# Two heads share two tiles by halves in a float32 encoder kernel

## The chip, the core and the metric

The kernel runs on one core of one Trainium2 chip. TensorE (PE in the profile; PEld is its weight load) multiplies, VectorE (DVE) and ScalarE (ACT) do the elementwise work, SyncE (SP) issues the transfers, GpSimd (POOL) does nothing here. Each engine runs its own list of instructions in order and waits on semaphores. The metric is the time of one execution on the device in microseconds (us), lower is better.

## The reference, cut to what matters

```python
for i in range(DEPTH):                       # DEPTH = 2 layers, 16 + 256 tokens, width 2048
    h = rms_norm(x, norm_w)
    proj = jnp.einsum('bld,dn->bln', h, w_in)            # one projection for all groups
    ya = diff_attention(aq, ak, av, ...)                 # branch A: 4 heads, two maps each
    yb = axial_gqa(bq, bk, bv, ...)                      # branch B: 4 q heads, 2 kv heads
    yc = latent_attention(cq, ckv, ckr, ...)             # branch C: low-rank latents
    yd = multiscale_pool(du, d_w_group, d_scale)         # branch D
    y = concat([ya * silu(ag), yb * silu(bg), yc * silu(cg), yd * silu(dg)])
    x = x + jnp.einsum('bln,nd->bld', y, w_out)

def axial_gqa(...):                          # heads of 128
    q, k = rms_norm(q_raw, q_norm_w), rms_norm(k_raw, k_norm_w)
    # rotary by halves: 0:64 by the grid row, 64:128 by the grid column;
    # apply_rope pairs element d with element d + 32 of its half (the partner)
    q, k = axial(q), axial(k)
    p = softmax32(q @ k, scale);  o = p @ v              # two q heads per kv head

def latent_attention(...):
    c_q, c_kv = rms_norm(cq_raw, q_lat_w), rms_norm(ckv_raw, kv_lat_w)
    q, kv = c_q @ w_uq, c_kv @ w_ukv                     # 4 heads, 128 nope + 64 rope
    q_nope, k_nope = rms_norm(q[..., :128], ...), rms_norm(kv[..., :128], ...)
    s = q_nope @ k_nope + q_rope @ k_rope                # then softmax and v
```

## The kernel before

Everything is kept transposed: features on the 128 partitions, the 272 tokens (`L`; 256 for queries and gates of the last layer) along the row. The big products (input projection, latent up-projections, output projection) are split by hand into a high and a low part of each factor, and `three` (lines 626 to 630) issues three matmuls for each product. Their weights come in chunks; ScalarE makes `w_hi` (`split`, L886), VectorE `w_lo` (`split`, L1162), three chunks ahead of TensorE. One chunk is 24 of these matmuls. A layer has 129 chunk slots: 23 column pairs of the input projection (4 slots each), 5 slots of up-projection behind the fourth pair, 8 output pairs.

A column pair of the projection gives two tiles of 128 features. ScalarE copies each out of PSUM (`lift`, L909), VectorE multiplies it by the inverse root of its token (`rescale`, L1170). Most tiles go to the two-tile buffer `row`. Then, for every tile with a norm of its own (`aq`, `ak`, `bq`, `bk`, and in branch C `qn`, `kn`, `qr`, `kr`):

- `rope_pre` on ScalarE squares the tile (`sq`, L949) and, for those that rotate, copies it with the norm weight (`qw`, L952);
- `rope_stat` on TensorE sums the squares over the partitions by a plain float32 matmul with a matrix of ones (`norm_ps`, L719) and, for those that rotate, fetches each element's partner by a matmul with a permutation (`swap_ps`, L724);
- `rope_fin` on ScalarE forms the inverse root (`rn`, L975 and L976), on VectorE rotates (L1182 to L1184) and multiplies by `rn` (L1191, or L1193 for `qn` and `kn`, which do not rotate).

The two latents are normalised by `lat_pre` (L959), `lat_stat` (L733: 3 matmuls for `cq`, 2 for `ckv`), `lat_fin` (L1206) and then split into `y_hi` (ScalarE, L1004) and `y_lo` (VectorE, L1200). A score step (`score`) makes two maps of 128 queries (or 16) by 272 keys. In branch A each map contracts 64 partitions (L764), m = 0 the lower half of the partitions and m = 1 the upper; in B each contracts 128 (L766); in C 128 (L768) and then 64 for the rotary part (L772). VectorE takes the maximum (L1273), ScalarE the exponential (L1039), VectorE divides (L1289, L1290), TensorE transposes (`p_turn`, L788) and multiplies by the values (`pv`, L807).

The order on each engine is written out by `make_plan`: a stage gets the number of a slot plus a fraction from a table of its engine (`AT_TENSOR`, `AT_SCALAR`, `AT_VECTOR`), and the engine runs its stages sorted by this sum. On TensorE `chunk` stands at 0.5 and `rope_stat` at 0.6, so a statistic of slot s follows the chunk of slot s, and the chunk of slot s + 1 is queued behind it. The latents' statistics stand at slots 12 and 13, those of `qn` 0, `kn` 0, `qr` 0, `qn` 1, `kn` 1, `qn` 2, ... from slot 22 on, one in each slot. Gates (`gate`: L1237, L1238, L1240) stand on VectorE at 0.336.

## Time and profile before

| | us |
|---|---|
| median of 3 runs | 961.72 (960.15 to 962.0) |
| the profiled execution, its time | 962.08 |
| its span in the profile | 960.3 |
| TensorE busy in it | 933.7 |
| VectorE busy in it | 689.0 |
| ScalarE busy in it | 577.9 |

The profiled execution lasted 0.4 us more than the median, and 1.8 us of it lie outside the span. TensorE's busy time has no large gap in any of 40 slices but the first and, a little, the last, and the granted clock is full in nearly all of them. An instruction of TensorE that is recorded as lasting 0.29 us is pipelined with its neighbours: what counts is the distance from one start to the next. A plain float32 matmul is recorded as two instructions.

### The profile page before, as it was taken

What the parts mean: (1) busy time and instruction counts of PE and PEld (TensorE: products, weight loads), DVE (VectorE), ACT (ScalarE), POOL (GpSimd) and SP (SyncE); (2) the same over time, 40 slices, a digit from 0 to 9 for tenths busy, and PEclk for the clock granted to TensorE, in tenths of its full rate; (3) what the DMA queues carried; (4) which work ended last, traced back from release to release, by engine and by line L of the source; (5) the groups of instructions that cost most, each with busy time, mean ns of one, the idle gap of its engine ahead of it and who ended that gap; (6) DMA issues with size and microseconds to landing.
All of it is one profiled execution on the core that took longest, in us unless ns stands there. A gap on an engine that the chain in (4) does not pass through costs nothing.

```text
span 960.3 us, 18378 instructions
## 1 busy us (share of the span) xinstructions
PE 933.7 (97%) x7144; PEld 891.2 (93%) x7144; DVE 689.0 (72%) x1100; ACT 577.9 (60%) x1038; POOL 0.2 (0%) x4
## 2 busy tenths in 40 slices
PE   6999999999999999999999999999999999999998
PEld 6998988999999989899999999999999999999998
DVE  6866986678687688876665568776787868787453
ACT  7577766557576665555554677665586575654331
POOL 0000000000000000000000000000000000000000
PEclk9999999999999999999999999999999999999999
DMA  9535332433333333344555354234434334334552
GB/s 345 218 133 189 119 130 89 136 128 132 132 132 132 132 114 125 114 176 175 177 187 176 132 176 176 92 129 146 148 125 154 132 133 172 126 111 174 200 181 91
DMA packets 22710, 143.84 MB, mean 150 GB/s; under 512 B 2528, under 2 KB 4576, under 8 KB 6240
## 3 DMA queue, kind: packets, MB, share of 16 engines
q1 hardware_dynamic: 22624, 142.67, 41.4%
q8 instruction: 57, 0.93, 0.4%
q14 instruction: 29, 0.24, 0.1%
HBM read 140.56 MB, written 2.10 MB: 149 GB/s over the span
## 4 chain that ended last, share of the span: by engine, by line
PE 83%; DVE 10%; ACT 5%; issue 1%; DMA 1%; SPq 0%; ACTq 0%; DVEq 0%
PE dense L628 23%; PE dense L630 23%; PE dense L629 23%; PE o_ps L807 4%; DVE gate_e L1238 3%; DVE w_lo L1162 3%; PE norm_ps L719 3%; PE swap_ps L724 2%; ACT w_hi L886 1%; PE t_ps L788 1%; PE s_ps L764 1%; PE s_ps L768 1%; ACT h_hi L867 1%; DVE stat L1273 1%; PE s_ps L772 1%
## 5 line engine op out<-in xcount | busy, mean ns | idle before, releaser
L628 PE MATMUL dense<-h_hi,w_hi 128*128 128x272 f32 (+1 forms) x1472 | 441.5, 300 | 11.8 <-DVE h_lo L1142 9.4
L630 PE MATMUL dense<-h_hi,w_lo 128*128 128x272 f32 (+1 forms) x1472 | 424.4, 288 | 0.0
L629 PE MATMUL dense<-h_lo,w_hi 128*128 128x272 f32 (+1 forms) x1472 | 422.4, 287 | 0.0
L1162 DVE TENSOR_TENSOR w_lo<-raw,w_hi 128x1024 fp32r<-128x1024 f32 (+1 forms) x258 | 314.5, 1219 | 73.7 <-ACT w_hi L886 66.8
L886 ACT ACTIVATE w_hi<-raw 128x1024 fp32r<-128x1024 f32 (+1 forms) x258 | 272.4, 1056 | 72.0 <-PE dense L630 62.2
L628 PEld LDWEIGHTS dense<-h_hi,w_hi 128*128 128x128 f32 x1472 | 279.4, 190 | 16.0 <-issue 10.6
L629 PEld LDWEIGHTS dense<-h_lo,w_hi 128*128 128x128 f32 x1472 | 279.8, 190 | 1.8
L630 PEld LDWEIGHTS dense<-h_hi,w_lo 128*128 128x128 f32 x1472 | 278.9, 189 | 0.0
L628 PE MATMUL dense<-y_hi,w_hi 128*128 128x272 f32 (+1 forms) x564 | 163.1, 289 | 3.6 <-DVE y_lo L1200 2.6
L630 PE MATMUL dense<-y_hi,w_lo 128*128 128x272 f32 (+1 forms) x564 | 162.6, 288 | 0.0
L629 PE MATMUL dense<-y_lo,w_hi 128*128 128x272 f32 (+1 forms) x564 | 162.2, 288 | 0.0
L628 PEld LDWEIGHTS dense<-y_hi,w_hi 128*128 128x128 f32 x564 | 108.0, 191 | 4.7 <-DVE y_lo L1200 3.0
L630 PEld LDWEIGHTS dense<-y_hi,w_lo 128*128 128x128 f32 x564 | 108.1, 192 | 0.0
L629 PEld LDWEIGHTS dense<-y_lo,w_hi 128*128 128x128 f32 x564 | 107.9, 191 | 0.0
L909 ACT ACTIVATE row<-dense 128x272 f32<-128x272 f32 (+1 forms) x80 | 31.5, 393 | 47.5 <-PE dense L630 46.2
L1238 DVE RECIPROCAL gate_e<-gate_e 128x272 f32<-128x272 f32 (+1 forms) x32 | 57.7, 1803 | 1.1
L975 ACT ACTIVATE rn<-norm_ps,eps_c 128x272 f32<-128x272 f32 (+1 forms) x64 | 31.0, 484 | 44.2 <-PE swap_ps L724 17.3
L1004 ACT ACTIVATE y_hi<-yt 128x256 fp32r<-128x256 f32 (+2 forms) x36 | 14.4, 400 | 69.5 <-DVE yt L1227 41.2
L1170 DVE TENSOR_TENSOR row<-row,rinv 128x272 f32<-128x272 f32 (+1 forms) x80 | 35.0, 437 | 25.5 <-ACT row L909 23.5
L807 PE MATMUL o_ps<-p_t,v_st 128*128 128x128 f32 (+1 forms) x360 | 47.3, 276 | 4.3 <-ACT p_t L1054 4.3
L807 PEld LDWEIGHTS o_ps<-p_t,v_st 128*128 128x128 f32 x360 | 45.2, 194 | 6.4 <-ACT p_t L1054 5.3
L1273 DVE TENSOR_REDUCE stat<-s_ps 128x1 f32<-128x272 f32 (+1 forms) x80 | 35.1, 439 | 21.8 <-PE s_ps L764 16.6
...
## 6 DMA issues: line engine op xcount, KB each, us to landing
raw<-w_stream_dram SPq DMA_DIRECT2D x128, 1024.0 KB, 4.8
...
con<-consts_dram SPq DMA_DIRECT2D x1, 320.0 KB, 12.7
...
```

Of the source, the lines that this page charges most:

```text
L628: nc.tensor.matmul(ps, whi, xhi, start=first, stop=False)
L629: nc.tensor.matmul(ps, whi, xlo, start=False, stop=False)
L630: return nc.tensor.matmul(ps, wlo, xhi, start=False, stop=last)
L719: sums = nc.tensor.matmul(norm_ps[:, t0:L], halves if width == 64 else ones, sq[:, parity("rope_stat", l, key, i), t0:L], start=True, stop ...
L807: mm = nc.tensor.matmul(o_ps[:, c:c + nq], v_st[:, b, 128 * vh:128 * vh + 128], p_t[:, m, 128 * b:128 * b + nq], start=b == 0, stop=b == 2)
L886: signal(nc.scalar.activation(w_hi[:, g % RING, 0:n], raw[:, e % RAW, CHUNK * half:CHUNK * half + n], ACT.Copy), hi_ready, g + 1)
L909: signal(nc.scalar.activation(tile_place(l, p, j), ps[:, 0:L - tile_from(l, kind)], ACT.Copy), lifted, scaled_no[(l, p, j)])
L975: link(nc.scalar.activation(rn[:, t0:L], norm_ps[:, t0:L], ACT.Ln, scale=1.0 / width, bias=eps_c[:, 0:1]))
L1162: signal(nc.vector.tensor_tensor(w_lo[:, g % RING, 0:n], raw[:, e % RAW, CHUNK * half:CHUNK * half + n], w_hi[:, g % RING, 0:n].bitcast(F3 ...
L1170: signal(nc.vector.tensor_tensor(out_, out_, rinv[:, tile_from(l, PAIRS[p][0]):L], ALU.mult), scaled, scaled_no[(l, p, j)])
L1238: link(nc.vector.reciprocal(e, e))
L1273: link(nc.vector.reduce_max(stat[0:nq, m:m + 1], s_ps[m][0:nq, 0:L], AX.X))
```

## The change

Two heads share two tiles by halves. For branch B and for `qn` and `kn` of branch C, the columns of the weights are reordered so that the first tile of a pair holds the first half of both heads (64 partitions each) and the second tile the second half; in B the halves are chosen so that an element and its rotary partner stand on the same partition of the two tiles. The two query heads that share a pair in B are 0 with 2 and 1 with 3 (`B_HEAD_AT`), one for each kv head. It follows:

- the partner matmul of B goes (`qw` and `swap_ps` too): VectorE rotates out of `row`, both tiles at once (`rope_mid`, three instructions over 2 x 272 columns);
- each pair has one square on ScalarE over both tiles, VectorE adds the two squared tiles (`sq_sum`), and one matmul with `halves` gives the sums of both heads. TensorE waits for the sum (semaphore `summed`) and no longer for the square. The latents' squares are added by VectorE too, two additions for `cq`, one for `ckv`, and one matmul each is left;
- `rope_fin` is one for each pair; in C its product stays two instructions;
- a score of B or C contracts 64 partitions at a time: the map of one head takes the lower half of the partitions of both tiles, the other the upper half. B has four such products in a step where it had two of 128, C six where it had two of 128 and two of 64;
- the list of C's stages is shorter (6 slots where it had 10). `sq_sum` stands at 0.2 of VectorE's table and `rope_mid` at 0.25; all other numbers stay;
- to make room, `gate_e` lies in `c_st[:, 4]` (a gate waits for the split of `ckv`), `acc` in `pooled`, and `sq` has four tiles. The lift behind `bq` and `bk` waits for `rotated`.

```diff
...
-AT_VECTOR = dict(s_max=-0.418, lam_dot=-0.35, sub_fin=-0.345, rope_fin=-0.34, lat_fin=0.055, head_out=0.17,
+AT_VECTOR = dict(sq_sum=0.2, rope_mid=0.25, s_max=-0.418, lam_dot=-0.35, sub_fin=-0.345, rope_fin=-0.34, lat_fin=0.055, head_out=0.17,
...
-                if kind in ("aq", "ak", "bq", "bk"):
+                if kind in ("aq", "ak"):
                     at(s, ("rope_pre", l, kind, i0 + j, j))
                     at(s, ("rope_stat", l, kind, i0 + j))
                     at(s + 1, ("rope_fin", l, kind, i0 + j))
+                elif kind in ("bq", "bk"):
+                    if j == 0:
+                        at(s, ("rope_pre", l, kind, i0 // 2, None))
+                        at(s, ("sq_sum", "rope", l, kind, i0 // 2))
+                        at(s, ("rope_mid", l, kind, i0 // 2))
+                        at(s, ("rope_stat", l, kind, i0 // 2))
+                        at(s + 1, ("rope_fin", l, kind, i0 // 2))
...
             at(s + n, ("lat_pre", l, key))
+            at(s + n, ("sq_sum", "lat", l, key))
             at(s + n, ("lat_stat", l, key))
             at(s + n + 1, ("lat_fin", l, key))
...
-        posts = [("qn", 0), ("kn", 0), ("qr", 0), ("qn", 1), ("kn", 1),
-                 ("qn", 2), ("kn", 2), ("qr", 1), ("qn", 3), ("kn", 3)]
+        posts = [("qn", 0), ("kn", 0), ("qr", 0), ("qn", 1), ("kn", 1), ("qr", 1)]
         for n, (key, i) in enumerate(posts):
             s = g0 + pair_slot(4) + 1 + n
             at(s, ("rope_pre", l, key, i, None))
+            if key in PAIRED:
+                at(s, ("sq_sum", "rope", l, key, i))
             at(s, ("rope_stat", l, key, i))
             at(s + 1, ("rope_fin", l, key, i))
...
-    sq = sb("sq", [128, 3, L])
+    sq = sb("sq", [128, 4, L])
     qw = sb("qw", [128, 2, L])
     rn = sb("rn", [128, L])
-    ta = sb("ta", [128, L + 16])
-    tb = sb("tb", [128, L + 16])
-    gate_e = sb("gate_e", [128, L])
+    tab = sb("tab", [128, 2, L + 16])
+    ta, tb = tab[:, 0, :], tab[:, 1, :]
+    gate_e = c_st[:, 4, :]
     pooled = sb("pooled", [128, L])
     probs = sb("probs", [128, 2, 2, L])
     p_t = sb("p_t", [128, 2, 3 * 128])
-    acc = sb("acc", [128, L])
+    acc = pooled
...
+    def pair_target(key, i):
+        return (q_st if key in ("bq", "qn") else k_st)[:, 2 * i:2 * i + 2, :]
+    def pair_source(key, i):
+        return row[:, :, 8:8 + L] if key in ("bq", "bk") else pair_target(key, i)
+    def twice(a, n):
+        return a.unsqueeze(1).broadcast_to([128, 2, n])
...
         def rope_stat(l, key, i):
-            branch, width = rope[key]
+            branch, _ = rope[key]
             t0 = rope_from(l, key)
-            pe.wait_ge(pre_done, pre_no[("rope_pre", l, key, i)])
+            if key in PAIRED:
+                pe.wait_ge(summed, sum_no[("rope", l, key, i)])
+            else:
+                pe.wait_ge(pre_done, pre_no[("rope_pre", l, key, i)])
             norm_free("rope_stat", l, key, i)
-            sums = nc.tensor.matmul(norm_ps[:, t0:L], halves if width == 64 else ones,
-                                    sq[:, parity("rope_stat", l, key, i), t0:L],
+            sums = nc.tensor.matmul(norm_ps[:, t0:L], halves, sq[:, 2 * parity("rope_stat", l, key, i), t0:L],
                                     start=True, stop=True)
             if branch:
                 swap_free("rope_stat", l, key, i)
             sums.then_inc(stat_done, 1)
         def lat_stat(l, key):
-            pe.wait_ge(pre_done, pre_no[("lat_pre", l, key)])
+            pe.wait_ge(summed, sum_no[("lat", l, key)])
             norm_free("lat_stat", l, key)
-            n = 3 if key == "cq" else 2
-            for k in range(n):
-                mm = nc.tensor.matmul(norm_ps[:, 0:L], ones, sq[:, k, :], start=k == 0, stop=k == n - 1)
-            mm.then_inc(stat_done, 1)
+            nc.tensor.matmul(norm_ps[:, 0:L], ones, sq[:, 0, :], start=True, stop=True).then_inc(stat_done, 1)
...
-            for m in (0, 1):
-                ps = s_ps[m][0:nq, 0:L]
-                if branch == "a":
-                    half = slice(64 * m, 64 * m + 64)
-                    mm = nc.tensor.matmul(ps, q_st[half, h, q:q + nq], k_st[half, h, :], start=True, stop=True)
-                elif branch == "b":
-                    mm = nc.tensor.matmul(ps, q_st[:, h + m, q:q + nq], k_st[:, h // 2, :], start=True, stop=True)
-                else:
-                    nc.tensor.matmul(ps, q_st[:, h + m, q:q + nq], k_st[:, h + m, :], start=True, stop=False)
+            if branch == "a":
+                parts = [(q_st[:, h, :], k_st[:, h, :])]
+            else:
+                k0 = h if branch == "c" else 0
+                parts = [(q_st[:, h, :], k_st[:, k0, :]), (q_st[:, h + 1, :], k_st[:, k0 + 1, :])]
             if branch == "c":
+                parts.append((c_st[:, 6 + h // 2, :], c_st[:, 5, :]))
+            for n_part, (queries, keys) in enumerate(parts):
                 for m in (0, 1):
                     half = slice(64 * m, 64 * m + 64)
-                    mm = nc.tensor.matmul(s_ps[m][0:nq, 0:L], c_st[half, 6 + h // 2, q:q + nq], c_st[half, 5, :],
-                                          start=False, stop=True)
+                    mm = nc.tensor.matmul(s_ps[m][0:nq, 0:L], queries[half, q:q + nq], keys[half, :],
+                                          start=n_part == 0, stop=n_part == len(parts) - 1)
             mm.then_inc(scores_ready, 1)
...
+                    elif pk in ("bq", "bk"):
+                        act.wait_ge(rotated, mid_no[(prev[0], pk, pi // 2)])
...
-            if key in ("qn", "kn", "qr"):
-                pass
-            else:
+            if key in ("bq", "bk"):
+                for t in (0, 1):
+                    act.wait_ge(scaled, scaled_of(l, key, 2 * i + t))
+            elif key not in ("qn", "kn", "qr"):
                 act.wait_ge(scaled, scaled_of(l, key, i))
             buffers_free("rope_stat", l, key, i)
             half = parity("rope_stat", l, key, i)
+            if key in PAIRED:
+                signal(nc.scalar.activation(sq[:, 2 * half:2 * half + 2, t0:L], pair_source(key, i)[:, :, t0:L],
+                                            ACT.Square), pre_done, pre_no[("rope_pre", l, key, i)])
+                return
             src = rope_source(key, i, j)[:, t0:L]
...
+            act.wait_ge(y_ready, y_count[(l, "ckv")])
...
+        def sq_sum(what, l, key, i=None):
+            n = sum_no[(what, l, key) if i is None else (what, l, key, i)]
+            if what == "lat":
+                dve.wait_ge(pre_done, pre_no[("lat_pre", l, key)])
+                if key == "cq":
+                    link(nc.vector.tensor_tensor(sq[:, 1, :], sq[:, 1, :], sq[:, 2, :], ALU.add))
+                signal(nc.vector.tensor_tensor(sq[:, 0, :], sq[:, 0, :], sq[:, 1, :], ALU.add), summed, n)
+                return
+            t0, half = rope_from(l, key), parity("rope_stat", l, key, i)
+            dve.wait_ge(pre_done, pre_no[("rope_pre", l, key, i)])
+            a, b = sq[:, 2 * half, t0:L], sq[:, 2 * half + 1, t0:L]
+            signal(nc.vector.tensor_tensor(a, a, b, ALU.add), summed, n)
+        def rope_mid(l, key, i):
+            t0 = rope_from(l, key)
+            n = L - t0
+            out_, t = pair_target(key, i)[:, :, t0:L], tab[:, :, t0:L]
+            tables = con[:, CC["neg_b"]:CC["neg_b"] + 3 * L].rearrange("p (a t) -> p a t", a=3)
+            x1, x2 = (twice(row[:, j, 8 + t0:8 + L], n) for j in (0, 1))
+            free = max(store_free(l, "b", key[-1], 2 * i + j) for j in (0, 1))
+            if free:
+                dve.wait_ge(scores_ready, free)
+            link(nc.vector.scalar_tensor_tensor(t, x1, pcol(l, key, 0), tables[:, 1:3, t0:L], ALU.mult, ALU.mult))
+            signal(nc.vector.scalar_tensor_tensor(out_, x2, pcol(l, key, 1), tables[:, 0:2, t0:L],
+                                                  ALU.mult, ALU.mult), rotated, mid_no[(l, key, i)])
+            link(nc.vector.tensor_tensor(out_, out_, t, ALU.add))
+        def pair_fin(l, key, i):
+            t0 = rope_from(l, key)
+            out_ = pair_target(key, i)[:, :, t0:L]
+            dve.wait_ge(rn_ready, norm_order[("rope_stat", l, key, i)] + 1)
+            if key in ("bq", "bk"):
+                last = nc.vector.tensor_tensor(out_, out_, twice(rn[:, t0:L], L - t0), ALU.mult)
+            else:
+                for j in (0, 1):
+                    o = out_[:, j, :]
+                    last = nc.vector.scalar_tensor_tensor(o, o, pcol(l, key, j), rn[:, t0:L], ALU.mult, ALU.mult)
+                    if j == 0:
+                        link(last)
+            signal(last, fin_done, fin_no[("rope_fin", l, key, i)])
...
-    put("cos_b", np.concatenate([cr, cc]))
-    put("sin_b", np.concatenate([sr, sc]))
+    put("cos_b", np.concatenate([cr[:32], cc[:32]] * 2))
+    put("sin_b", np.concatenate([sr[32:], sc[32:]] * 2))
+    put("neg_b", np.concatenate([sr[:32], sc[:32]] * 2))
...
+            elif kind in ("bq", "bk", "bg"):
+                heads = [wi[:, :, OFF[kind] + 128 * h:OFF[kind] + 128 * h + 128]
+                         for h in ((0, 1) if kind == "bk" else B_HEAD_AT[i:i + 2])]
+                cols = np.concatenate(heads if kind == "bg" else [h[:, :, d] for d in B_HALVES for h in heads], axis=2)
...
```

What this moves on VectorE is read at three places. In all of them `sq<-sq` (L1213, L1214, L1219) is the sum that TensorE waits for.

First place: VectorE at the two latent norms of layer 0 (slots 12 and 13), before: the latents' rescale, two chunks' `w_lo`, the product of `cq`, its low part, a chunk, the same for `ckv`.

```order
L1170 TENSOR_TENSOR c_st<-c_st,rinv 128x272 x2
L1162 TENSOR_TENSOR w_lo<-raw,w_hi 128x1024 x2
L1206 SCALAR_TENSOR_TENSOR c_st<-c_st,par,rn 128x272 x3
L1200 TENSOR_TENSOR y_lo<-c_st,y_hi 128x816
L1162 TENSOR_TENSOR w_lo<-raw,w_hi 128x768
L1206 SCALAR_TENSOR_TENSOR c_st<-c_st,par,rn 128x272 x2
L1200 TENSOR_TENSOR y_lo<-c_st,y_hi 128x544
```

The same place after:

```order
L1204 TENSOR_TENSOR c_st<-c_st,rinv 128x272 x2
L1196 TENSOR_TENSOR w_lo<-raw,w_hi 128x1024
L1213 TENSOR_TENSOR sq<-sq 128x272
L1214 TENSOR_TENSOR sq<-sq 128x272
L1196 TENSOR_TENSOR w_lo<-raw,w_hi 128x1024
L1283 SCALAR_TENSOR_TENSOR c_st<-c_st,par,rn 128x272 x3
L1277 TENSOR_TENSOR y_lo<-c_st,y_hi 128x816
L1214 TENSOR_TENSOR sq<-sq 128x272
L1196 TENSOR_TENSOR w_lo<-raw,w_hi 128x768
L1283 SCALAR_TENSOR_TENSOR c_st<-c_st,par,rn 128x272 x2
L1277 TENSOR_TENSOR y_lo<-c_st,y_hi 128x544
```

Two additions stand behind the first `w_lo`, the sum for `ckv` behind the low part of `cq`, which itself waits for ScalarE's `y_hi`.

Second place: VectorE at the norms of `qn` 0 and `kn` 0 in layer 0 (slots 21 to 23), before: a gate, a chunk, then products and chunks in turn.

```order
L1237 TENSOR_SCALAR gate_e<-gate_e 128x272
L1238 RECIPROCAL gate_e<-gate_e 128x272
L1240 TENSOR_TENSOR g_st<-row,gate_e 128x272
L1162 TENSOR_TENSOR w_lo<-raw,w_hi 128x1024
L1193 SCALAR_TENSOR_TENSOR q_st<-q_st,par,rn 128x272
L1162 TENSOR_TENSOR w_lo<-raw,w_hi 128x1024
L1193 SCALAR_TENSOR_TENSOR k_st<-k_st,par,rn 128x272
L1162 TENSOR_TENSOR w_lo<-raw,w_hi 128x1024
```

After, with the gate's buffer now in `c_st`:

```order
L1314 TENSOR_SCALAR c_st<-c_st 128x272
L1315 RECIPROCAL c_st<-c_st 128x272
L1317 TENSOR_TENSOR g_st<-row,c_st 128x272
L1196 TENSOR_TENSOR w_lo<-raw,w_hi 128x1024
L1219 TENSOR_TENSOR sq<-sq 128x272
L1246 SCALAR_TENSOR_TENSOR q_st<-q_st,par,rn 128x272 x2
L1196 TENSOR_TENSOR w_lo<-raw,w_hi 128x1024
L1219 TENSOR_TENSOR sq<-sq 128x272
L1246 SCALAR_TENSOR_TENSOR k_st<-k_st,par,rn 128x272 x2
L1196 TENSOR_TENSOR w_lo<-raw,w_hi 128x1024
```

Each sum stands behind a chunk's `w_lo`, and that behind the two products of the pair before.

Third place: VectorE at `bk` in layer 1 (and alike at the first `bq` of layer 1), before: rescale, the end of a head of branch A (L1216, L1218), a chunk, the low part of that head, the rotation.

```order
L1170 TENSOR_TENSOR row<-row,rinv 128x272 x2
L1216 SCALAR_TENSOR_TENSOR ta<-o_ps,sub_w,rn 128x256
L1218 TENSOR_TENSOR yt<-ta,g_st 128x256
L1162 TENSOR_TENSOR w_lo<-raw,w_hi 128x1024
L1200 TENSOR_TENSOR y_lo<-yt,y_hi 128x256
L1182 TENSOR_TENSOR ta<-swap_ps,con 128x272
L1183 TENSOR_TENSOR tb<-qw,con 128x272
L1184 TENSOR_TENSOR tb<-tb,ta 128x272
L1191 TENSOR_TENSOR k_st<-tb,rn 128x272
L1162 TENSOR_TENSOR w_lo<-raw,w_hi 128x1024
```

After:

```order
L1204 TENSOR_TENSOR row<-row,rinv 128x272 x2
L1293 SCALAR_TENSOR_TENSOR tab<-o_ps,sub_w,rn 128x256
L1295 TENSOR_TENSOR yt<-tab,g_st 128x256
L1196 TENSOR_TENSOR w_lo<-raw,w_hi 128x1024
L1277 TENSOR_TENSOR y_lo<-yt,y_hi 128x256
L1219 TENSOR_TENSOR sq<-sq 128x272
L1231 SCALAR_TENSOR_TENSOR tab<-row,par,con 128x2x272
L1232 SCALAR_TENSOR_TENSOR k_st<-row,par,con 128x544
L1234 TENSOR_TENSOR k_st<-k_st,tab 128x544
L1242 TENSOR_TENSOR k_st<-k_st,rn 128x544
```

The sum takes the place of the rotation's first instruction, behind the chunk and the head's low part. For the other four pairs of B the sum stands directly behind a chunk.

## Rows read from the trace of the kernel before

**Rows 1.** The page: span, and busy time of the engines.
```profile
span 960.3 us, 18378 instructions
...
PE 933.7 (97%) x7144; PEld 891.2 (93%) x7144; DVE 689.0 (72%) x1100; ACT 577.9 (60%) x1038; POOL 0.2 (0%) x4
...
```

**Rows 2.** The page, chain that ended last: shares of the span.
```profile
...
PE 83%; DVE 10%; ACT 5%; issue 1%; DMA 1%; SPq 0%; ACTq 0%; DVEq 0%
...
```

**Rows 3.** Chain in order of time: start, us, engine, tile, line, instructions merged.
```profile
...
53.16 1.37 PE norm_ps L733 x6
...
86.58 0.46 PE norm_ps L719 x2
...
107.92 0.92 PE s_ps L768 x4
108.84 0.66 PE s_ps L772 x4
109.50 0.66 PE norm_ps L719 x2
...
```

**Rows 4.** Timeline, latent norms, layer 0: start, us, engine, line [idle before <-releaser].
```profile
...
51.83 1.23 DVE L1162 TENSOR_TENSOR w_lo<-raw,w_hi 128x1024 fp32r<-128x1024 f32 x1 [0.66 <-ACT w_hi L886]
...
53.00 1.54 PE L733 MATMUL norm_ps<-sq,con 128*128 128x272 f32 x6
...
57.36 0.88 ACT L1004 ACTIVATE y_hi<-c_st 128x816 fp32r<-128x816 f32 x1 [1.07 <-DVE c_st L1206]
57.40 1.08 PE L733 MATMUL norm_ps<-sq,con 128*128 128x272 f32 x4
...
58.34 1.01 DVE L1200 TENSOR_TENSOR y_lo<-c_st,y_hi 128x816 fp32r<-128x816 f32 x1 [1.08 <-ACT y_hi L1004]
...
```

**Rows 5.** Timeline, a gate and the norms of qn and kn, layer 0.
```profile
...
84.01 1.85 DVE L1238 RECIPROCAL gate_e<-gate_e 128x272 f32<-128x272 f32 x1
...
86.38 1.23 DVE L1162 TENSOR_TENSOR w_lo<-raw,w_hi 128x1024 fp32r<-128x1024 f32 x1
86.42 0.62 PE L719 MATMUL norm_ps<-sq,con 128*128 128x272 f32 x2
...
88.18 0.50 DVE L1193 SCALAR_TENSOR_TENSOR q_st<-q_st,par,rn 128x272 f32<-128x272 f32 x1 [0.58 <-ACT rn L976]
...
88.72 1.23 DVE L1162 TENSOR_TENSOR w_lo<-raw,w_hi 128x1024 fp32r<-128x1024 f32 x1
...
89.90 0.62 PE L719 MATMUL norm_ps<-sq,con 128*128 128x272 f32 x2
...
```

**Rows 6.** Timeline, first tile of bk, layer 1.
```profile
...
756.02 0.73 PE L719 MATMUL norm_ps<-sq,con 128*128 128x272 f32 x2 [0.15 <-ACT qw L952]
756.03 1.22 DVE L1162 TENSOR_TENSOR w_lo<-raw,w_hi 128x1024 fp32r<-128x1024 f32 x1
...
757.29 0.42 DVE L1200 TENSOR_TENSOR y_lo<-yt,y_hi 128x256 fp32r<-128x256 f32 x1
...
```

**Rows 7.** Stretches: each engine's busy us (instructions), then PEclk, DMA share, GB/s.
```profile
...
374.00:380.00 6.00, 4.66 (x35) 4.11 (x34) 5.69 (x10) 3.33 (x8) 0.00 (x0) 1.00 0.51 178
399.50:401.50 2.00, 0.17 (x2) 0.00 (x0) 1.90 (x4) 1.57 (x6) 0.00 (x0) 1.00 0.01 4
...
404.00:406.00 2.00, 2.00 (x11) 2.00 (x10) 1.24 (x5) 1.31 (x3) 0.00 (x0) 0.50 0.51 213
406.00:408.00 2.00, 2.00 (x14) 2.00 (x13) 1.97 (x2) 0.41 (x1) 0.00 (x0) 0.75 0.00 0
...
```

**Rows 8.** Groups by form: instructions, busy us, mean ns, idle before.
```profile
...
L1184 DVE TENSOR_TENSOR tb<-tb,ta 128x272 f32<-128x272 f32 x24 | 10.6, 442 | 0.8
...
L1193 DVE SCALAR_TENSOR_TENSOR k_st<-k_st,par,rn 128x272 f32<-128x272 f32 x8 | 4.0, 502 | 6.8 <-ACT rn L976 6.8
...
L1105 DVE TENSOR_TENSOR q_st<-q_st 128x544 f32<-128x544 f32 x1 | 0.7, 728 | 0.0
...
```

**Rows 9.** Waits in total, TensorE: us, times, longest.
```profile
...
PE t_ps L788 <- DVE probs L1290: 2.5, 2, 1.3
...
```

76 lines of the change are left out of this document (43 added, 33 removed).

## The prediction, made before the changed kernel was run

> **What bounds the kernel now.** I read the page first: TensorE is busy for 933.7 of 960.3 us, and the chain of work that ended last lies on it for 83% of the span [rows 1, 2]. VectorE has 72%. So a microsecond of TensorE is worth a microsecond of time, nearly everywhere, and so is a microsecond in which TensorE is made to wait. I then read the chain in order of time for the prices of the small matmuls, the timeline for where VectorE stands when TensorE reaches a statistic, and the windows for the places where TensorE has waited before. The reader should see in the timeline rows that ScalarE's squares are ready when TensorE comes: its statistic follows its chunk with no idle time but once, 0.15 us [rows 4 to 6]. VectorE is at that moment in the middle of a `w_lo` of 1.23 us, or about to begin one. That is the place where the new sum comes in.
>
> **Prices on TensorE.** Three float32 matmuls of 128 by 272 take 1.37 us in the chain, a single one 0.46 us [rows 3]. A pair of half-height matmuls, m = 0 and m = 1, costs 0.66 us; the statistic behind it then takes 0.66 us in place of 0.46, so a pass of halves costs 0.66 + 0.20 = 0.86 us, which I split into 0.46 us for the pass (the two halves run beside each other) and 0.40 us for going in and out of that mode [rows 3].
>
> **What goes on TensorE.** Latents: `cq` 3 to 1 matmuls, `ckv` 2 to 1, 3 x 0.46 = 1.4 us a layer. Branch C: 8 statistics become 4, 4 x 0.46 = 1.8 us a layer. Branch B: a pair had 4 matmuls (two statistics, two partners) and has 1, so 1.38 us for each of 6 pairs, 8.1 us in all, since one kind has only 256 columns in the last layer. Together 2.8 + 3.7 + 8.1 = 14.6 us in both layers.
>
> **What the scores cost.** In C a step had 0.92 + 0.66 + 0.20 = 1.78 us [rows 3]. After, it has three passes of halves and one switch, 3 x 0.46 + 0.40 = 1.78 us: nothing gained. In B a step had 0.92 us and gets 2 x 0.46 + 0.40 = 1.32 us, 0.40 us more, in 10 steps 4.0 us. About half of these stand ahead of a place where TensorE then waits for `probs` anyway (TensorE is busy for 4.66 of 6.00 us there, longest wait 1.3 us [rows 7, 9]), so I take 2.0 us, with 0 and 4.0 as ends. If halves don't run beside each other when both come from new tiles, each pass costs a second 0.46 us, which is the worst end; the four instructions in 0.66 us of the same form speak against it [rows 3].
>
> **VectorE and ScalarE themselves.** ScalarE sheds the copies `qw` and has fewer fixed starts; it has 60% and stays hidden. VectorE's work for a pair of B: before, two times four instructions of 0.44 us, 3.5 us; after, one sum of 0.44, two products of 544 columns and two simple ones. The only row of 544 columns is 0.73 us, against 0.44 for 272 [rows 8], so with 0.79 us for the two-scalar form (0.50 against 0.44 at 272 columns) it is 0.44 + 2 x 0.79 + 2 x 0.73 = 3.5 us: no change. In C and in the latents it gains 4 and 3 sums a layer, 7 x 0.44 = 3.1 us, on an engine that is idle for a quarter of the time. As volume this is nothing. As order it is all that counts: the sums stand in VectorE's list behind work that is timed for a later chunk, and TensorE waits for them with its next chunk of 24 matmuls queued behind.
>
> **The new waits: latents.** `cq`: TensorE reaches the statistic at 53.00. VectorE began its `w_lo` at 51.83 and ends it at 53.06; two sums of 0.44 and a signal of some 0.1 us bring it to 54.05. Wait 1.05 us [rows 4]. `ckv`: TensorE came at 57.40, and comes at about 57.5 now (0.92 less, 1.05 more). The sum stands behind the low part of `cq`, which waits for ScalarE's `y_hi` and began at 58.34, lasting 1.01 us; with the shift of 0.1 it ends at 59.5, the sum makes it 60.0. Wait 2.5 us [rows 4]. Two layers: 2 x 3.55 = 7.1 us. The low end is 2 x 1.5, if ScalarE, relieved, brings `y_hi` forward by a microsecond.
>
> **The new waits: `qn` and `kn`.** `qn` 0: TensorE at 86.42, VectorE's `w_lo` from 86.38 to 87.61, sum to 88.1. Wait 1.7 us [rows 5]. From there a loop closes, each turn through both engines: from a statistic to the product that needs its root is 88.18 - 86.42 = 1.76 us; two products, 1.07; the next `w_lo`, 1.27 with its gap; the sum, 0.5: 4.6 us from one statistic to the next sum. TensorE's own turn is 89.90 - 86.42 = 3.48 us [rows 5]. So `kn` 0 waits 1.1 us. By the same steps through the table of VectorE, `qn` 1 waits 1.3 us (behind the rotation of `qr`), `kn` 1, behind a gate with its reciprocal of 1.85 us [rows 5], 2.0 us. Sum 6.1 us a layer, 12.2 in both, against 3.7 us saved. Ends: 3 us a layer if the gate comes earlier, 7.5 if a gate falls on two of them.
>
> **The new waits: branch B.** `bk` in layer 1: TensorE is there at 756.02; VectorE runs `w_lo` from 756.03 for 1.22 us, the head's low part (from 757.29) for 0.42, then the sum, ready at 758.2. Wait 2.2 us [rows 6]. The first `bq` of that layer stands alike: 4.4 us. At the other four pairs the sum follows a chunk directly: between 0, where VectorE has time in hand, and 1.7 us (`w_lo` starting just then, then the sum). I take 0.4 us each, since these chunks' `w_lo` had mostly begun well before TensorE arrived: 1.6 us. Together 6.0 us.
>
> **Sum without the clock.** -14.6 + 2.0 + 7.1 + 12.2 + 6.0 = +12.7 us, on the profiled execution's own 962.1 us: 974.8. The median of the runs is 0.4 us lower, which I neglect.
>
> **The clock.** After TensorE had been idle for 1.83 of the 2.00 us from 399.5 to 401.5, its granted clock was 0.50 in 404 to 406 and 0.75 in 406 to 408, which is the level of 1.2 GHz in place of 2.4 for 3 of those 4 us. That costs 1.0 + 0.5 = 1.5 us. In 374 to 380, with waits up to 1.3 us, it stayed at 1.00 [rows 7, 9]. Of my waits four lie at 2.2 to 2.5 us (`ckv` twice, `bk` and the first `bq` in layer 1), so four falls, 4 x 1.5 = 6 us: 974.8 + 6 = 980.8, rounded to **981**.
>
> The Trainium skill ("TensorE: Matmul & The Clock Gate", the section on HAM oscillation) warns of idle gaps longer than any wait in this list, so by its rule none of them costs clock, and the time would be that of the rival without falls. The trace's fall behind a stall of 2.0 us speaks against it.
>
> **Rivals.** (1) *The same waits and no falls*: the stall before 401.5 is one of several close together, and a single wait between full chunks may not be enough to lower the clock. 974.8 us. For it: the other waits here are embedded in dense work. (2) *The waits of 1.7 and 2.0 us lower it too*: two in each layer, 4 x 1.5 more: 987 us. For it: the stall that did was hardly longer, 1.83 us in that window. (3) *Waits partly given back*: TensorE's chunk was itself at times late for `w_lo`, and the relieved ScalarE runs `w_hi`, roots and `y_hi` earlier, so that VectorE's `w_lo` is done before TensorE comes at half of these places. Halving the 25.3 us of waits gives 962.1 - 14.6 + 2.0 + 12.7 = 962 without a fall; a third given back, 16.9 us left, and one fall give 968, and I take 968. (4) *The other sign: the sums are not awaited*. VectorE has idle time before its `w_lo` (0.66 us before that of 51.83, released by ScalarE's `w_hi` [rows 4]). If ScalarE's lead grows so much that VectorE runs a whole chunk ahead, every sum is ready, as ScalarE's squares are now. It decides at a lead of about 2 us over the rows above; then 962.1 - 14.6 + 2.0 = 949.5, with small rests 951 us. Against it: sums stand behind `w_lo` by the table, and VectorE follows `w_hi`, which ScalarE makes only as the buffers come free from TensorE's own chunks. (5) *That the change doesn't do what it says*, a half-height pass at the price of two, adds 0.46 us to each of the 2 new passes of a step of B and C, 20 steps, 18 us: 999. Four such instructions in 0.66 us leave it 1 in 50.
>
> **How the numbers follow.** Forecast 43%, no falls 20%, more falls 17%, partly given back 10%, never awaited 8%, halves at double price 2%. The likeliest gives 981. The range goes from just below the rival at 968 to just above that at 987: 966 to 988. Some 0.2% (2 us) is about what a measurement of this kernel can tell from no change. Faster by more than that is the case of 951 and the lowest part of the one given back: 9%; within it 2%; slower 89%.
>
> **What would show it.** In the profile after: waits of TensorE's statistics (`norm_ps`) on VectorE's `sq`, some 14 to 16 a time with 20 to 25 us together, where none stood; the longest at `ckv`, over 2 us in both layers. TensorE's busy time lower by 10 to 14 us (longer if the clock falls are counted), its share nearer 94%. A granted clock under full within 4 us behind `ckv` and behind `bk` of layer 1. The chain's score pieces of C unchanged near 1.8 us with its switch, those of B near 1.3. Then VectorE's share of the chain above 10%. The prediction is wrong if those waits are under 10 us in all, if they hit only where the table puts a gate, or if TensorE's chunks between them close up faster than 3.48 us a turn, which would mean that they had been waiting for something that this change relieves.

## The result, and the profile after

| | before | after |
|---|---|---|
| median of the runs, us | 961.65 (4 runs, 960.15 to 962.0) | 977.8 (4 runs, 976.05 to 978.95) |
| the profiled execution, us | 962.08 | 976.05 |
| its span, us | 960.3 | 974.2 |

The ratio is 1.0167, 95% interval 1.0153 to 1.018: the change makes the kernel 16 us slower. The forecast was 981, the range 966 to 988. The execution that was profiled is the fastest of the four, and its span is 13.9 us longer than that of before.

The page of the changed kernel gives the span, the busy time of the engines, and the chain that ended last by engine:

```profile
span 974.2 us, 18313 instructions
...
PE 926.5 (95%) x7160; PEld 882.7 (91%) x7160; DVE 694.8 (71%) x1096; ACT 557.1 (57%) x984; POOL 0.2 (0%) x4
...
PE 70%; DVE 20%; ACT 7%; issue 2%; DMA 1%; ACTq 0%; SPq 0%; DVEq 0%
```

TensorE works 7.2 us less than before and the whole takes 13.9 us more, so it stands idle for 21.1 us more [rows 1]. VectorE's share of the chain has doubled from 10 to 20% [rows 2]. Its own busy time has hardly moved (689.0 to 694.8 us), so it is not more work that brought it there.

TensorE's waits by what ended them (us in total, times, longest):

```profile
PE norm_ps L751 <- DVE sq L1219: 16.0, 12, 2.5
PE dense L657 <- DVE h_lo L1176: 8.9, 1, 8.9
PE norm_ps L762 <- DVE sq L1214: 6.2, 4, 2.5
PE o_ps L833 <- ACT p_t L1088: 4.3, 3, 2.0
...
PE t_ps L814 <- DVE probs L1367: 1.3, 2, 0.7
```

The first and the third row did not exist before: 16 waits for a sum of VectorE, 22.2 us. The wait for `probs` fell from 2.5 to 1.3 us [rows 9], which is where part of the scores' extra time went.

The timeline of the first `ckv` wait in layer 0 (matmuls of the chunk left out):

```profile
55.40 0.66 ACT L992 ACTIVATE sq<-c_st 128x544 f32<-128x544 f32 x1
55.47 1.58 DVE L1283 SCALAR_TENSOR_TENSOR c_st<-c_st,par,rn 128x272 f32<-128x272 f32 x3 [0.67 <-ACT rn L1009]
...
57.14 0.88 ACT L1037 ACTIVATE y_hi<-c_st 128x816 fp32r<-128x816 f32 x1 [1.08 <-DVE c_st L1283]
...
58.13 1.01 DVE L1277 TENSOR_TENSOR y_lo<-c_st,y_hi 128x816 fp32r<-128x816 f32 x1 [1.08 <-ACT y_hi L1037]
59.17 0.44 DVE L1214 TENSOR_TENSOR sq<-sq 128x272 f32<-128x272 f32 x1
...
59.67 0.72 PE L762 MATMUL norm_ps<-sq,con 128*128 128x272 f32 x2 [2.33 <-DVE sq L1214]
```

This answers to [rows 4]. The square for `ckv` had been ready since 56.06 (55.40 + 0.66, the first row). The sum, which takes 0.44 us, waits three microseconds for its turn. It stands behind the products of `cq` and its `y_lo`, and for one of these microseconds VectorE itself waits for ScalarE's `y_hi`. The loop through the pairs of C (answering to [rows 5]):

```profile
88.27 1.22 DVE L1196 TENSOR_TENSOR w_lo<-raw,w_hi 128x1024 fp32r<-128x1024 f32 x1
...
89.53 0.44 DVE L1219 TENSOR_TENSOR sq<-sq 128x272 f32<-128x272 f32 x1
...
90.03 0.73 PE L751 MATMUL norm_ps<-sq,con 128*128 128x272 f32 x2 [1.55 <-DVE sq L1219]
...
91.90 1.04 DVE L1246 SCALAR_TENSOR_TENSOR q_st<-q_st,par,rn 128x272 f32<-128x272 f32 x2 [1.92 <-ACT rn L1009]
...
92.97 1.22 DVE L1196 TENSOR_TENSOR w_lo<-raw,w_hi 128x1024 fp32r<-128x1024 f32 x1
...
93.48 0.29 PE L659 MATMUL dense<-h_hi,w_lo 128*128 128x272 f32 x1
94.23 0.44 DVE L1219 TENSOR_TENSOR sq<-sq 128x272 f32<-128x272 f32 x1
...
94.72 0.72 PE L751 MATMUL norm_ps<-sq,con 128*128 128x272 f32 x2 [0.96 <-DVE sq L1219]
```

From statistic to statistic it is now 94.72 - 90.03 = 4.69 us, where it was 3.48. The last three rows also show how a wait is measured: neighbouring matmuls of a chunk start 0.13 us apart though each is recorded as 0.29 us, so from 93.48 the next could have started at 93.61, and the wait is 1.11 us, not the 0.96 that is shown as idle. Measured like this, the waits of the profile are 24.8 us, not 22.2.

### The profile page after: what moved, and what is told of

Same layout as the page of the kernel before. It is cut to its first block, busy times and chain, and to the rows that moved or that the text cites. A ratio compares the mean times of both kernels' runs of the same rounds, so it can differ in the third digit from the quotient of the medians.

```text
span 974.2 us, 18313 instructions
## 1 busy us (share of the span) xinstructions
PE 926.5 (95%) x7160; PEld 882.7 (91%) x7160; DVE 694.8 (71%) x1096; ACT 557.1 (57%) x984; POOL 0.2 (0%) x4
## 4 chain that ended last, share of the span: by engine, by line
PE 70%; DVE 20%; ACT 7%; issue 2%; DMA 1%; ACTq 0%; SPq 0%; DVEq 0%
PE dense L657 20%; PE dense L659 20%; PE dense L658 19%; DVE w_lo L1196 6%; DVE c_st L1315 4%; PE o_ps L833 3%; PE s_ps L798 3%; ACT w_hi L912 2%; PE norm_ps L751 2%; DVE stat L1350 1%; PE t_ps L814 1%; PE swap_ps L755 1%; ACT h_hi L893 1%; DVE row L1204 1%; DVE g_st L1317 1%
## 5 line engine op out<-in xcount | busy, mean ns | idle before, releaser
L1315 DVE RECIPROCAL c_st<-c_st 128x272 f32<-128x272 f32 (+1 forms) x32 | 57.7, 1803 | 1.1
L1008 ACT ACTIVATE rn<-norm_ps,eps_c 128x272 f32<-128x272 f32 (+1 forms) x50 | 24.3, 486 | 52.2 <-PE norm_ps L751 21.9
L1073 ACT ACTIVATE probs<-s_ps,stat 128x272 f32<-128x272 f32 (+1 forms) x80 | 39.0, 487 | 26.0 <-DVE stat L1351 23.5
```

The costliest lines, as they stand in the source:

```text
L1073: signal(nc.scalar.activation(probs[0:nq, k % 2, m, :], s_ps[m][0:nq, 0:L], ACT.Exp, bias=stat[0:nq, 2 + m:3 + m], scale=SCALE[b], accum_o ...
L1315: link(nc.vector.reciprocal(e, e))
```

## The experiments

**Where the sum stands.** First everything that the sums need is put earlier, with the same arithmetic:

```
+    if name == "sq_sum":
...
+        return -0.05 if key == "ckv" else -0.545
+    if name in ("rope_pre", "lat_pre") and stage[2] in EARLY:
+        return 0 if stage[2] == "ckv" else (-0.41 if name == "rope_pre" else -0.397)
...
-            plan.append((slot + at_engine[kind] + MOVED.get(stage, 0), len(plan), stage))
+            plan.append((slot + at_engine[kind] + MOVED.get(stage, 0) + early(stage), len(plan), stage))
```

> Edit: the changed kernel, with every square of a pair (and of cq) moved on ScalarE to just before the w_hi of the slot before, and every sum on VectorE to just before the w_lo of the slot before; for ckv the sum goes only ahead of the low part of cq. The arithmetic is the same. Theory (TensorE waits because of the sum's place in VectorE's list): its waits of 22.2 us on the sums go nearly to nothing and the clock falls behind them too, so 977.8 - 22 - 2 = 954, up to 959 if VectorE and ScalarE now wait for each other ahead of a chunk. Rival (the pair is late as such, through the square over both tiles and the sum itself, wherever they stand): most of the waits stay, 970 or more.

Measured: 958.59 us, ratio to before 0.9968 (0.9954 to 0.9982). The same work in another order is 19 us faster than the changed kernel and a little faster than the kernel before. Its waits of TensorE:

```profile
PE norm_ps L766 <- DVE sq L1234: 2.6, 4, 0.9
...
PE norm_ps L777 <- DVE sq L1229: 1.8, 2, 1.1
```

22.2 us became 4.4, in six places. The largest that are left have work of 1.6 to 2.3 us ahead of them that was not moved: at `ckv` the three products of `cq` (1.58 us), and at `kn` 1 VectorE's gate. This is the place ahead of the sum of `kn` 1, in the timeline of this kernel:

```profile
98.59 1.85 DVE L1330 RECIPROCAL c_st<-c_st 128x272 f32<-128x272 f32 x1
...
100.48 0.44 DVE L1332 TENSOR_TENSOR g_st<-row,c_st 128x272 f32<-128x272 f32 x1
100.96 0.44 DVE L1234 TENSOR_TENSOR sq<-sq 128x272 f32<-128x272 f32 x1
...
101.45 0.72 PE L766 MATMUL norm_ps<-sq,con 128*128 128x272 f32 x2 [0.87 <-DVE sq L1234]
```

With them, and with 1.3 us of waits for `rn` that are new, it comes out at the upper end of what was expected. The view of waits has more of the kind: those for ScalarE's `p_t` grew from 4.3 to 5.8 us and those for its `c_st` from 1.3 to 2.1. It looks as if the squares that ScalarE now makes a slot earlier push back its other work; this comes up again below.

**No sum at all.** VectorE's sum goes and the matmul accumulates over the squared tiles:

```
+ON_PE = ('cq', 'ckv', 'qn', 'kn', 'bq', 'bk')
...
-            sums = nc.tensor.matmul(norm_ps[:, t0:L], halves, sq[:, 2 * parity("rope_stat", l, key, i), t0:L],
-                                    start=True, stop=True)
+            tiles = (0, 1) if key in ON_PE else (0,)
+            for n in tiles:
+                sums = nc.tensor.matmul(norm_ps[:, t0:L], halves, sq[:, 2 * parity("rope_stat", l, key, i) + n, t0:L],
+                                        start=n == 0, stop=n == tiles[-1])
```

> Edit: the changed kernel without any sum on VectorE; TensorE adds the squared tiles itself, in one accumulation of two matmuls for a pair, three for cq and two for ckv, and waits for ScalarE's square as before the change. 10 matmuls more in a layer. Theory (place of the sum): the waits of 22.2 us go, 20 x 0.46 = 9.2 us of matmuls come, 977.8 - 22 + 9 - 2 = 963, range 960 to 966. Rival (the square over both tiles is late): the waits only change their releaser from the sum to the square, 975 or more.

Measured: 955.85 us, 0.9948 (0.9932 to 0.9964). The same kernel a second time, as tensor_again below, took 954.49 (0.9929, 0.9917 to 0.9941). No statistic waits for anything. This was 7 us under my expectation, outside its range. Comparing the start of each chunk in the two traces shows why. At `ckv` in layer 0 this kernel gains 2.13 us, where the wait of 2.49 less a matmul of 0.46 gives 2.03, and about 0.1 us more (0.09 to 0.19) appears at the other places too: the first matmuls behind a wait start that much further apart. I call this the restart. With 24.8 us from start to start in place of the 22 that I had taken from the view, 1.6 us of restarts, and 4.2 us of clock where I had put 2, the sum is 24.8 + 1.6 + 4.2 - 9.2 = 21.4 us, and the two spans are 974.2 and 952.8. The 4.2 us are what closes this sum; the starts of the chunks behind the falls give about 4 by themselves (see the clock, further down).

**Is it VectorE's sum that ends the waits?** The last addition is done twice:

```
+            link(nc.vector.tensor_tensor(yt_x[:, t0:L], a, b, ALU.add))
             signal(nc.vector.tensor_tensor(a, a, b, ALU.add), summed, n)
```

> Edit: the changed kernel; VectorE does the last addition of each sum once more, into a tile nobody reads, ahead of the real one: 0.44 to 0.5 us more in front of each of 16 waits. Theory: each of the twelve long waits grows by the whole of it, the four short ones of branch B by a part, 5.5 to 7.5 us, and one or two more clock falls of 1.7 us: 985, range 982 to 990. Rival (VectorE is not what ends these waits, it only stands next to it): 978 to 980.

Measured: 987.35 us, 1.0279 (1.026 to 1.0298). Its two rows:

```profile
PE norm_ps L752 <- DVE sq L1222: 23.4, 14, 3.0
...
PE norm_ps L763 <- DVE sq L1216: 8.1, 4, 3.0
```

The waits of layer 0 grew from 1.06, 2.49, 1.72, 1.12, 1.29 and 1.92 us to 1.53, 2.96, 2.19, 1.58, 1.76 and 2.41: each by 0.46 to 0.49, that is by the whole of the added instruction. In total 34.3 us against 24.8. The rival is refuted: VectorE's sum ends these waits.

**One part alone: the latents.** The kernel before, with VectorE's sums for `cq` and `ckv` and nothing else:

```
...
-            for k in range(n):
-                mm = nc.tensor.matmul(norm_ps[:, 0:L], ones, sq[:, k, :], start=k == 0, stop=k == n - 1)
-            mm.then_inc(stat_done, 1)
+            nc.tensor.matmul(norm_ps[:, 0:L], ones, sq[:, 0, :], start=True, stop=True).then_inc(stat_done, 1)
...
+            signal(nc.vector.tensor_tensor(sq[:, 0, :], sq[:, 0, :], sq[:, 1, :], ALU.add), summed,
+                   2 * l + (key == "ckv") + 1)
```

> Edit: the kernel before, with one part of the change alone: VectorE adds the squares of the latents, at 0.2 of its table, and one matmul is left for each. Theory (place of the sum): the same waits as in the changed kernel, about 1.06 and 2.5 us a layer, with 0.1 us of restart each, against 3 x 0.46 us of matmuls saved: (3.55 + 0.2 - 1.4) x 2 = +4.7, so 966 with the kernel before at 961.3, range 965 to 968.5 with a clock fall. Rival (the long waits come only with the other parts of the change, which load ScalarE and VectorE differently): matmuls saved and no wait, 958.5.

Measured: 966.96 us, 1.0056 (1.0034 to 1.0079), beside 961.7 of before. The waits are 1.06 and 2.48 us in layer 0, 0.64 and 2.67 in layer 1, those of the changed kernel to 0.02 us. So these waits need nothing of the other parts. Three matmuls a layer were saved for it.

**One part taken back: `qn` and `kn`.** The changed kernel with the second matmul for these four statistics a layer only; the code is that of sums_on_tensor with another list:

```
-ON_PE = ('cq', 'ckv', 'qn', 'kn', 'bq', 'bk')
+ON_PE = ('qn', 'kn')
```

> Edit: the changed kernel; the sums of qn and kn alone are made on TensorE by a second matmul each (8 in both layers), the latents' and B's stay on VectorE. Theory: the waits of C in the changed kernel (6.0 us in layer 0, 5.2 in layer 1, with 8 x 0.1 us of restart) and about two clock falls of 1.5 us go, 8 x 0.46 us come: 978 - 12 - 3 + 3.7 = 966.7, range 964.5 to 969, since the falls that are left may hit another wait. Rival (the waits of C are the tail of an earlier delay by the latents, and only move): the waits at bk and bq of layer 1 grow, 971 or more.

Measured: 965.4 us, 1.004 (1.0025 to 1.0054). The waits of C are gone; those of the latents (1.06, 2.48, 0.64, 2.63) and of B in layer 1 (2.54, 2.69) stand as they were, to 0.02 us. Of B's three waits in layer 0 one went from 0.60 to 0.56 and one from 0.59 to 0.38 us. So the parts add up, and hardly hand their delay on.

**The new form of the scores.** The kernel before, with B's scores as four matmuls over 64 partitions:

```
+            if branch == "b":
+                for part in (0, 1):
+                    for m in (0, 1):
+                        half = slice(64 * m, 64 * m + 64)
+                        mm = nc.tensor.matmul(s_ps[m][0:nq, 0:L], q_st[half, h + m, q:q + nq],
+                                              k_st[half, h // 2, :], start=part == 0, stop=part == 1)
```

> Edit: the kernel before, with the scores of branch B alone in the new form: four matmuls over 64 partitions a step in place of two over 128. Both passes read the same half of a head, so the product over the other half is left out and its output is not the reference's. Theory: 0.40 us more on TensorE in 10 steps, 4.0 us, partly swallowed by the waits for probs behind them: +2, range 0 to +4 on the kernel before, 962 to 966. Rival (halves of full heads don't run beside each other): a further 0.46 us for each pass, +11 or more, over 972.

Measured: 962.21 us beside 961.28, 1.0011 (1.0002 to 1.0021), +0.9 us. The chain of this kernel has the step as

```profile
328.96 1.12 PE s_ps L778 x8
...
336.32 1.12 PE s_ps L778 x8
```

and 0.2 us of switching behind it: 1.31 us for the step, as estimated (1.32). So of 4.0 us on TensorE at most about 1 reaches the end, and part of that can be the clock: these ten runs have a mean granted clock of 0.993 to 0.996, the fifteen of before 0.993 to 1.000, and the runs at 0.996 in both (two and seven) differ by 0.4 us. Some of the rest goes where TensorE waited anyway: in this kernel, too, the waits for `probs` fell from 2.5 to 1.3 us. What takes the remainder was not traced.

**Whether a wait lowers the clock.** The changed kernel a second time, and once with all that follows put 1.8 us later:

```
-            nc.tensor.matmul(norm_ps[:, 0:L], ones, acc[:, :], start=True, stop=True).then_inc(stat_done, 1)
+            for _ in range(1 if l else 5):
+                mm = nc.tensor.matmul(norm_ps[:, 0:L], ones, acc[:, :], start=True, stop=True)
+            mm.then_inc(stat_done, 1)
```

> The changed kernel once more, unaltered, for a second profiled execution: its waits of TensorE on the sums should stand as before, 24.8 us from start to start, and the time near 978. Theory P (whether a wait of 1.9 to 2.7 us lowers the granted clock depends on when it happens, not on the place alone): new falls appear at some of the seven such waits, not at the same three (110, 584 and 770 us). Rival L (the place decides): falls at the same three waits, within 0.3 us.

> Edit: the changed kernel; the first statistic over the input is issued five times in place of once in layer 0, which moves all that follows by 4 x 0.46 = 1.8 us and alters nothing else. Theory P (the moment decides): the waits stay as long as they are, and the set of places where the clock falls changes against the unaltered kernel of this job; time 978 + 1.8, plus or minus one fall of 1.5 us. Rival L (the place decides): falls behind the same waits, 1.8 us later, and 979.6.

Measured: 978.1 us (1.0175, 1.015 to 1.02) and 979.2 us (1.0183, 1.0163 to 1.0203). All waits are the same in the three traces, within 0.05 us. The places where the granted clock falls to 0.50 differ. Windows of the first profiled execution (busy us and instructions of each engine, then granted clock, DMA share, GB/s):

```profile
60.00:62.00 2.00, 2.00 (x17) 1.96 (x16) 1.07 (x2) 1.42 (x4) 0.00 (x0) 1.00 0.00 0
110.00:112.00 2.00, 2.00 (x10) 2.00 (x10) 0.88 (x2) 1.87 (x4) 0.00 (x0) 0.50 0.85 352
...
556.00:558.00 2.00, 2.00 (x17) 1.96 (x17) 1.04 (x3) 1.72 (x4) 0.00 (x0) 1.00 0.00 0
584.00:586.00 2.00, 2.00 (x9) 1.82 (x9) 0.15 (x1) 1.12 (x3) 0.00 (x0) 0.50 0.78 238
770.00:776.00 6.00, 4.90 (x25) 4.82 (x26) 5.22 (x8) 2.42 (x4) 0.00 (x0) 0.72 0.00 0
```

and of after_again:

```profile
60.00:62.00 2.00, 1.83 (x8) 1.75 (x9) 1.07 (x2) 0.95 (x3) 0.00 (x0) 0.69 0.00 0
112.00:114.00 2.00, 2.00 (x18) 2.00 (x17) 1.01 (x2) 1.87 (x5) 0.00 (x0) 1.00 0.77 315
...
556.00:558.00 2.00, 2.00 (x12) 2.00 (x11) 1.00 (x2) 1.73 (x4) 0.00 (x0) 0.50 0.00 0
586.00:588.00 2.00, 2.00 (x13) 1.98 (x12) 0.57 (x2) 1.55 (x3) 0.00 (x0) 0.61 0.83 262
772.00:778.00 6.00, 5.12 (x26) 4.95 (x26) 5.04 (x7) 2.20 (x4) 0.00 (x0) 0.72 0.00 0
```

| wait | us | after | after_again | after_shifted |
|---|---|---|---|---|
| `ckv`, layer 0 | 2.49 | full | falls | falls |
| `kn` 1, layer 0 | 1.92 | falls | full | falls |
| `ckv`, layer 1 | 2.65 | full | falls | full |
| `qn` 0, layer 1 | 1.95 | falls | falls | falls |
| `bk`, layer 1 | 2.54 | falls | falls | falls |
| first `bq`, layer 1 | 2.69 | full | full | full |

Three rows change from one execution to another of the same waits, so the moment has a part in it. Three rows do not change in these three traces, but two other kernels with waits at the same places do otherwise there. In c_on_tensor the wait for `bk` is the same 2.54 us, ends at 760.4, and the clock stays full:

```profile
760.00:764.00 4.00, 3.61 (x26) 3.46 (x26) 3.83 (x6) 1.98 (x3) 0.00 (x0) 1.00 0.00 0
```

In sum_twice the clock falls behind `bq` (3.14 us) and not behind `qn` 0 of layer 1 (2.36 us). So no place is bound to its fall or spared from it. Now all waits for a sum in the six traces that have long ones (the three above, sum_twice, latent_sums_alone and c_on_tensor), from start to start: of those up to 1.87 us none was followed by a fall, of the 28 from 1.9 to 2.7 us half were (14), and of the four above (2.96, 3.01, 3.12 and 3.14 us, in sum_twice) all. What decides within the middle group beyond the moment stays open.

**Which sums are worth keeping.** Two mixtures. The statistics in a list are made on TensorE as in sums_on_tensor, all others on VectorE, early, as in sums_early:

```
+def on_tensor(l, key, i=0):
+    return (l, key, i) in ON_TENSOR
...
+        return 0 if key in ON_TENSOR else -0.41 if name == "rope_pre" else -0.397
```

In mixed the list holds `ckv`, `qn` 0 and `kn` 1 of both layers, `bk` and the first `bq` of layer 1; in two_sums all but `kn` 0 and `qn` 1.

> Edit: the changed kernel; the sums that were still awaited in sums_early (ckv, qn 0 and kn 1 in both layers, bk and the first bq in layer 1) are made on TensorE by a second matmul, the others (cq, kn 0, qn 1, the other four pairs of B) on VectorE at the earlier place with the square moved too. Theory: against sums_on_tensor 2 x 0.92 + 4 x 0.46 + 4 x 0.46 = 5.5 us of matmuls less and still no wait, 955.9 - 5.5 = 950.4, up to 953 if the square's earlier place holds up w_hi. Rival (TensorE's chunks are by now as fast as w_lo comes, so what is saved turns into other waits): 955 or more.

Measured: 954.9 us, 0.9934 (0.9916 to 0.9951). The expectation failed, the rival was nearer. In the traces, chunk by chunk against sums_on_tensor, the saved matmuls are there (0.92 us at `cq` of layer 0, 0.46 at `kn` 0 and at `qn` 1), but behind `cq` TensorE loses 0.44 us a slot later, and behind the early squares of B and of `cq` in layer 1 0.57, 0.63 and 0.61 us at one place each. 5.5 us saved left 0.5, and 0.4 of that is an earlier start of the first chunk. What the rest turned into stands in the views of waits, here of mixed and then of two_sums, the next kernel:

```profile
PE o_ps L860 <- ACT p_t L1115: 5.8, 6, 2.0
PE dense L676 <- ACT c_st L964: 2.1, 2, 1.4
PE norm_ps L772 <- ACT qw L1012: 0.8, 2, 0.7
```

```profile
PE o_ps L860 <- ACT p_t L1115: 4.3, 3, 2.0
PE dense L676 <- ACT c_st L964: 1.5, 1, 1.5
```

The waits for ScalarE's `p_t` and `c_st` are those of sums_early again (5.8 and 2.1), and the one for `qw` was not there in sums_on_tensor. So the rival came near in the number, but not for its reason: the view has no wait for `w_lo`, the new ones are for ScalarE. That fits its early squares of `cq` and of B standing ahead of its other work, for two_sums, which moves neither, has hardly any of this; no run moved those squares alone.

> Edit: as sums_on_tensor, but the sums of kn 0 and qn 1 are made on VectorE at the earlier place, with the square moved too; in mixed these four places showed no wait and each saved 0.46 us, while the early squares of cq and B brought waits of 0.4 to 0.6 us in other places. Theory: 4 x 0.46 = 1.8 us under sums_on_tensor of this job. Rival (a matmul saved there is given back behind it): no difference to it.

> The kernel of sums_on_tensor once more, unaltered, in more rounds, as the one that two_sums is compared with: 955.9 expected, 0.994 to 0.996 of the kernel before.

Measured side by side: two_sums 951.92 us, 0.9898 (0.9884 to 0.9911), tensor_again 954.49 (a little under what was expected of it). The chunks of two_sums start earlier by some 0.43 to 0.5 us behind exactly the four statistics. Of the other 2.3 us between the two profiles 0.35 are the start of the first chunk and 1.9 arise near the ends of the layers, where their clock falls differ. The medians differ by 2.6 us for the 1.8 expected, and part of this too is the clock: two_sums ran at a mean of 0.995 to 1.000, tensor_again at 0.993 to 0.999, and runs at nearly the same clock differ by 1.6 us (0.995 and 0.996) and 2.0 us (0.998 or more). This is the fastest kernel of the study, 1.0% faster than before and 2.7% faster than the change as made. Its page:

```profile
span 949.8 us, 18347 instructions
...
PE 924.7 (97%) x7192; PEld 883.0 (93%) x7192; DVE 687.8 (72%) x1080; ACT 556.3 (59%) x984; POOL 0.2 (0%) x4
```

## Why the prediction was right

**The side and the size came from the waits.** Forecast and measured, in us, from start to start:

| sum | forecast | layer 0 | layer 1 |
|---|---|---|---|
| `cq` | 1.05 | 1.06 | 0.65 |
| `ckv` | 2.5 | 2.49 | 2.65 |
| `qn` 0 | 1.7 | 1.72 | 1.95 |
| `kn` 0 | 1.1 | 1.12 | under 0.2 |
| `qn` 1 | 1.3 | 1.29 | 1.41 |
| `kn` 1 | 2.0 | 1.92 | 1.80 |
| `bk`, first `bq`, layer 1 | 2.2 each | | 2.54, 2.69 |
| other four of B | 0.4 each | 0.58, 0.60, none | 0.31 |

Together 25.3 and 24.8 us. In layer 0 those of the latents and of C could be worked out to a tenth because the rows of before already held every instruction ahead of the sum with its start [rows 4, 5]; at B the error was 0.1 to 0.5 us. That the totals lie 0.5 us apart is partly luck: in layer 1 `cq` and `kn` 0 came out about 1.5 us under the forecast, and the other seven together about 1.1 us over it. At `kn` 0 in layer 1 there was no wait since TensorE was still at half clock behind the wait of `qn` 0 and came late itself; in sum_twice, where the clock did not fall at `qn` 0, `kn` 0 waits 1.70 us.

**The matmuls saved and the scores** were forecast at -14.6 + 2.0 = -12.6 us. Measured: sums_on_tensor, which has 9.2 us of these matmuls left in, is 7.5 us shorter in span than before, so this part is -16.7. The prices held: C's step cost the same as before, B's 1.31 us for 1.32. What was mis-sized is the scores' part that comes through, 0.9 us at most for 2.0 (half_scores_alone). Of the other 3 us, 0.7 are two old waits for `qw` that went [rows 6]. Some 1.4 are no saved work at all: 0.5 is the start of the first chunk, which differs that much between executions, and 0.9 stand at the end of layer 1, where the profile of before has two falls of the clock and that of sums_on_tensor one. The last 0.9 us I have not traced.

**The restarts**, 16 x 0.1 = 1.6 us, are a term that the prediction did not have.

**The clock** was forecast at four falls of 1.5 us, 6 us. The profiled execution has three new ones, one at a place that was named (`bk`) and two that were not (`kn` 1 of layer 0, `qn` 0 of layer 1), and none at the other three named (`ckv` twice, `bq`). They cost 1.5 us each in the chunks behind them, 4.6 us in all; 4.2 net, since one fall at the end of layer 1 that sums_on_tensor has is missing here. Against the kernel before it is less still, for there two are missing. Its windows, and those of the same two stalls in the changed kernel:

```profile
854.00:858.00 4.00, 4.00 (x23) 4.00 (x22) 2.46 (x5) 1.93 (x4) 0.00 (x0) 0.57 0.58 236
874.00:878.00 4.00, 3.85 (x20) 3.85 (x21) 2.27 (x5) 3.05 (x4) 0.00 (x0) 0.58 0.03 8
```

```profile
869.00:873.00 4.00, 4.00 (x34) 4.00 (x35) 2.20 (x4) 2.07 (x4) 0.00 (x0) 1.00 0.77 266
888.00:892.00 4.00, 2.60 (x20) 2.42 (x21) 2.72 (x5) 3.87 (x5) 0.00 (x0) 1.00 0.07 23
```

From these two stalls on, the chunks of the changed kernel catch up by 1.5 us. Between the two profiles the clock is therefore worth about 3 us and not 6: three new falls against two old ones that did not come, and as far as these traces show, which of them come is chance. The mean granted clock says the same, 0.994 before and 0.993 after. The prediction had looked at one old fall, the one at 404, as a price, and not asked whether the old falls would come again. Its reason was only half right as well: I took the length of the wait as what decides, at 2.0 to 2.2 us, and waits of 1.92 us lowered the clock where one of 2.69 did not. The other three runs of this kernel lasted 1.2 to 2.9 us longer than the profiled one, at a mean granted clock of 0.989 to 0.991 against its 0.993; at 1.5 us a fall this is one or two falls more.

Sum for the span: -16.7 + 24.8 + 1.6 + 4.2 = +13.9 us. The forecast's was +18.7. The 4.8 us between them are 4.1 in the first term, 1.8 in the clock, and 1.1 the other way in waits and restarts. Of the 4.1 only some 2.7 are work that was worth more than I had put; the rest is the start and the falls named above. The forecast of 981 lies 3.2 us over the median of 977.8, in which errors of both signs have cancelled, so its nearness is in part luck. What holds without luck is the side and the 24.8 us of waits that set it.

**The rivals.** "No falls" (974.8) was as near in the number as the forecast (3.0 us off against 3.2) and wrong in its reason: new falls are in all three profiles of these waits. "More falls" (987) needed falls behind waits of 1.7 and 2.0 us; there was none behind 1.72 and 1.80, and some behind 1.92 and 1.95. "Partly given back" did not happen: 24.8 of 25.3 us of waits stayed, though ScalarE was relieved (577.9 to 557.1 us busy). "Never awaited" (951) did not occur as the change was made; sums_early shows what it would have taken: once the square and the sum stand ahead of `w_lo`, 18 of the 22 us go. Halves at double price is refuted by half_scores_alone.

Most of what the prediction named as signs came out: 16 waits with 22.2 us in the view of waits (20 to 25 forecast), the longest at `ckv` and B, VectorE's share of the chain at 20%, and the scores of B at 1.31 us in half_scores_alone. The lowered clock came behind `bk` of layer 1 but not behind `ckv`. TensorE's busy time fell by 7.2 us and not by 10 to 14, since the half-clocked stretches and the scores count in it, and its share is 95%, not 94.
